# Relevance products behind the first six projections, the key search begun between them, and the bias matrix read back with a row step

## What is computed

```python
def block(i):
    ...
    rel = jax.nn.relu(jnp.einsum("bqhe,bse->bqhs", qi, k_idx).astype(jnp.float32))
    score = jnp.einsum("bqhs,bqh->bqs", rel, wi)
    ...
    score = jnp.where(causal[None], score, -jnp.inf)
    _, idx = lax.top_k(score, n_sel)
    ...
    bias = rel_bias[_t5_bucket(t[None, :, None] - idx)]
    logits = logits + jnp.transpose(bias, (0, 3, 1, 2)).astype(jnp.float32)
```

## Time and profile before

| | us |
|---|---|
| median of 3 runs | 2497.31 (2497.22 to 2499.72) |
| the profiled execution's span | 2496.9 |
| TensorE busy | 2376.4 (95%) |
| VectorE busy | 831.4 (33%) |
| ScalarE busy | 728.9 (29%) |
| GpSimd busy | 682.1 (27%) |

### The profile page before, as it was taken

One profiled execution on the slowest core, in us unless ns is written; L12 is line 12 of the kernel. 1 busy time (PEld: TensorE's weight loads), 2 busy tenths in 40 slices (PEclk: granted clock), 3 DMA queues, 4 the chain that ended last, 5 costly groups with the idle time before them and its releaser, 6 DMA issues.

```text
span 2496.9 us, 29386 instructions
## 1 busy us (share of the span) xinstructions
PE 2376.4 (95%) x11620; PEld 1715.4 (69%) x11620; DVE 831.4 (33%) x1298; ACT 728.9 (29%) x1089; POOL 682.1 (27%) x366
## 2 busy tenths in 40 slices
PE   7999999979999999989999999999999999999998
PEld 5585445753333347855899999979777677878875
DVE  2653412341111232350274054145000443721722
ACT  3324433321111211354142122232322334322222
POOL 3140012511111001110134444424433034544541
PEclk9699999989999999999999999999999999999999
DMA  4121111547899522200122222222222022322220
GB/s 152 60 93 59 46 37 40 229 165 273 356 358 380 237 68 72 76 18 9 59 85 85 93 86 84 93 85 94 93 85 76 18 75 69 101 85 97 97 89 38
DMA packets 68315, 275.41 MB, mean 110 GB/s; under 512 B 12488, under 2 KB 12616, under 8 KB 55920
## 3 DMA queue, kind: packets, MB, share of 16 engines
q1 hardware_dynamic: 59408, 259.61, 29.2%
q0 software_dynamic: 8512, 13.89, 1.6%
q10 hardware_dynamic: 288, 0.40, 0.1%
HBM read 321.02 MB, written 16.80 MB: 135 GB/s over the span
## 4 chain that ended last, share of the span: by engine, by line
PE 88%; issue 4%; DVE 3%; ACT 2%; POOL 2%; DMA 0%; DVEq 0%; POOLq 0%; SPq 0%; ACTq 0%
PE ps L826 16%; PE ps L809 15%; PE ps L1244 7%; PE ps L795 6%; PE ps L1016 4%; PE ps L1059 3%; PE ps L496 3%; PE ps L1266 3%; PE ps L1119 2%; PE ps L1205 2%; PE ps L707 2%; POOL weights_low L2473 2%; PE ps L1043 2%; PE ps L627 2%; PE ps L507 2%
## 5 line engine op out<-in xcount | busy, mean ns | idle before, releaser
L2473 POOL TENSOR_TENSOR weights_low<-weights,parts 128x1024 fp32r<-128x1024 f32 x218 | 547.3, 2513 | 988.4 <-ACT parts L1736 988.4
L826 PE MATMUL ps<-parts 128*128 128x512 f32 x1344 | 419.6, 392 | 9.2 <-DVE parts L2004 6.8
L809 PE MATMUL ps<-parts 128*128 128x264 f32 x2240 | 411.3, 285 | 8.1 <-DVE parts L2004 6.9
L1736 ACT ACTIVATE parts<-weights 128x1024 fp32r<-128x1024 f32 x218 | 229.1, 1055 | 440.4 <-PE ps L809 145.0
L809 PEld LDWEIGHTS ps<-parts 128*128 128x128 f32 x2240 | 349.6, 190 | 8.8 <-issue 8.7
L809 PE MATMUL ps<-parts,weights_low 128*128 128x264 f32 x1120 | 319.3, 285 | 0.0
L826 PEld LDWEIGHTS ps<-parts 128*128 128x128 f32 x1344 | 253.8, 189 | 66.1 <-issue 10.4
L826 PE MATMUL ps<-parts,weights_low 128*128 128x512 f32 x672 | 263.6, 392 | 0.0
L809 PEld LDWEIGHTS ps<-parts,weights_low 128*128 128x128 f32 x1120 | 213.1, 190 | 0.0
L1244 PE MATMUL ps<-area,normed 128*64 128x512 f32 x752 | 171.3, 597 | 1.6 <-DVE normed L2191 1.6
L2004 DVE TENSOR_TENSOR parts<-normed,parts 128x528 f32 (+1 forms) x64 | 152.2, 2378 | 10.1 <-DVE normed L2003 2.7
(11 more groups left out here) (419 smaller groups left out, 3307.7 us busy)
## 6 DMA issues: line engine op xcount, KB each, us to landing
weights<-in_weights SPq DMA_DIRECT2D x283, 512.0 KB, 3.4
area<-in_experts SPq DMA_DIRECT2D x141, 1024.0 KB
area<-pair_rows SPq DMA_DIRECT2D x4, 1024.0 KB, 8.1
residual<-in_x SPq DMA_DIRECT2D x4, 512.0 KB, 7.2
area<-bias_scratch POOLq DMA_DIRECT2D x1, 2048.0 KB, 9.7
token_rows<-area SPq DMA_DIRECT2D x1, 2048.0 KB, 6.6
out_tiles<-residual SPq DMA_DIRECT2D x4, 512.0 KB, 2.8
area<-in_decay POOLq DMA_DIRECT2D x2, 528.0 KB, 3.7
```

The costliest lines, as they stand in the source:

```text
L809: ins = mm(ps[:, b + h, 0:HALF], wt[:, k], x[:, m * DT + k, HALF * h:HALF * h + HALF], start=m == k == j == 0, stop=m == chunks - 1 and k ...
L826: ins = mm(ps[:, b], wt[:, k], x[:, m * DT + k, first:first + SEQ], start=m == k == j == 0, stop=m == chunks - 1 and k == DT - 1 and j == 2)
L1736: fn(high_slot(n, place), RING[:, n % SLOTS], ACT.Copy).then_inc(S["w_hi"], 1)
L2473: g.tensor_tensor(RING_LOW[:, n % SLOTS], RING[:, n % SLOTS], high_slot(n, place), ALU.subtract).then_inc(S["w_lo"], 1)
```

## The change

Five things change. The relevance products (`relevance`, four per call) stand behind the projections 1 to 6 of the twelve; they use banks 4 to 7 and four tiles `REL`. ScalarE's ReLUs stand behind the high part of the same turn. VectorE puts 5 rounds of the search for t = 1 behind its scoring steps 12, 16 and 20, and before the first of them waits for `bias_rows` and for the mask of t = 1. The bias vectors are written to DRAM from ScalarE's queue, each 128 times (`bias_scratch` is 8 x 128 x 640), and GpSimd reads the matrix from them with a step of 639 values from row to row, right into `BIAS`, so the reversed identity, its products and their copies are gone. And GpSimd makes the low parts of chunks 8 and 9 ahead of its wait for the write, those of 10 to 15 between its masks.

```diff
@@ -195,14 +195,14 @@
-        REL = [area(TMP, 512), area(TMP + 512, 512)]
+        REL = [area(TMP + 512 * j, 512) for j in range(4)]
...
-        BIAS_FLIPPED = area(5120, HEADS, SEQ)
-
+        RELS = [(t, h) for t in range(1, QT) for h in range(HEADS)]
+        EACH = 4
@@ -325,7 +325,7 @@
-        bias_scratch = nc.dram_tensor("bias_scratch", (HEADS, BIAS_W), F32, kind="Internal")
+        bias_scratch = nc.dram_tensor("bias_scratch", (HEADS, P, BIAS_W), F32, kind="Internal")
@@ -540,26 +540,13 @@
                              RELB, HOT[:, j * (BIAS_W // 2):(j + 1) * (BIAS_W // 2)], start=True, stop=True)
                 ins.then_inc(S["bias_vec"], 1)
 
-                if w.counted("act_evac"):
-                    pe.wait_ge(S["act_evac"], w.value("act_evac"))
-                for n, (t, h) in enumerate((t, h) for t in range(1, QT) for h in range(HEADS)):
-                    if n == 0:
+                begin_stage("act_evac")
+                for c in range(12):
+                    linear_split(HH, HL, IN_FIRST)
+                    if c == 0:
                         pe.wait_ge(S["bias_dram"], w.next("bias_dram", 1))
-                    if n >= 2:
-                        pe.wait_ge(S["rel_sb"], w.next("rel_sb"))
-                    r = slice(HD * (h % 2), HD * (h % 2) + HD)
-                    mm(ps[:, 4 + n % 2, 0:P * (t + 1)], QI[r, h // 2, P * t:P * t + P], KI[r, 0:P * (t + 1)],
-                       start=True, stop=True).then_inc(S["rel_done"], 1)
-                pe.wait_ge(S["rel_sb"], w.next("rel_sb", 2))
-                pe.wait_ge(S["bias_rows"], w.next("bias_rows", 16))
-                for h in range(HEADS):
-                    if h >= 2:
-                        pe.wait_ge(S["bias_flip"], w.next("bias_flip"))
-                    mm(ps[:, 4 + h % 2], FLIP, BIAS_FLIPPED[:, h], start=True, stop=True).then_inc(S["flip_done"], 1)
-                pe.wait_ge(S["bias_flip"], w.next("bias_flip", 2))
-                begin_stage("act_evac")
-                for _ in range(12):
-                    linear_split(HH, HL, IN_FIRST)
+                    relevance(range(EACH * c, min(EACH * c + EACH, len(RELS))))
+                pe.wait_ge(S["rel_sb"], w.next("rel_sb", 4))
                 banks = [bank() for _ in range(QT)]
                 for m in range(4):
                     wh, wl = (x.rearrange("p k c -> p (k c)") for x in take_parts(IN_FIRST))
@@ -779,6 +766,16 @@
                 pe_mlp(linear_tokens, [(0, 0, SEQ)], (XH1, XL1), (FH1, FL1))
                 layer_norm(TOKENS)
 
+            def relevance(turns):
+
+                for n in turns:
+                    t, h = RELS[n]
+                    r = slice(HD * (h % 2), HD * (h % 2) + HD)
+                    if n >= 4:
+                        pe.wait_ge(S["rel_sb"], w.next("rel_sb"))
+                    mm(ps[:, 4 + n % 4, 0:P * (t + 1)], QI[r, h // 2, P * t:P * t + P], KI[r, 0:P * (t + 1)],
+                       start=True, stop=True).then_inc(S["rel_done"], 1)
+
             def linear2(chunks, rhs, kts, fresh=None, late=False):
 
                 b = 2 * bank()
@@ -1348,18 +1345,18 @@
                 act.wait_ge(S["bias_vec"], w.next("bias_vec"))
                 fn(BVEC[:, 0:BIAS_W // 2], ps[0:HEADS, 6, 0:BIAS_W // 2], ACT.Copy)
                 fn(BVEC[:, BIAS_W // 2:], ps[0:HEADS, 5, 0:BIAS_W // 2], ACT.Copy).then_inc(S["bias_dram"], 1)
-                for n, (t, h) in enumerate((t, h) for t in range(1, QT) for h in range(HEADS)):
-                    act.wait_ge(S["rel_done"], w.next("rel_done"))
-                    if n >= 2:
-                        act.wait_ge(S["rel_used"], w.next("rel_used"))
-                    fn(REL[n % 2][:, 0:P * (t + 1)], ps[:, 4 + n % 2, 0:P * (t + 1)], ACT.Relu).then_inc(S["rel_sb"], 1)
-                w.count("rel_used", 2)
-                for h in range(HEADS):
-                    act.wait_ge(S["flip_done"], w.next("flip_done"))
-                    fn(BIAS[:, h], ps[:, 4 + h % 2], ACT.Copy).then_inc(S["bias_flip"], 1)
+                act.wait_ge(S["bias_dram"], 1)
+                act.dma_start(bias_scratch.ap(), BVEC.unsqueeze(1).to_broadcast([HEADS, P, BIAS_W])).then_inc(S["bvec_out"], 16)
                 for n, out in enumerate([x[:, j] for x in (QA, QB, KB) for j in range(4)]):
                     evac(out, bank(n), scale=QK_SCALE if n < 8 else 1.0)
                     high(n + 8, place=IN_FIRST, slots=-1)
+                    for m in range(EACH * n, min(EACH * n + EACH, len(RELS))):
+                        act.wait_ge(S["rel_done"], w.next("rel_done"))
+                        if m >= 4:
+                            act.wait_ge(S["rel_used"], w.next("rel_used"))
+                        keys = P * (RELS[m][0] + 1)
+                        fn(REL[m % 4][:, 0:keys], ps[:, 4 + m % 4, 0:keys], ACT.Relu).then_inc(S["rel_sb"], 1)
+                w.count("rel_used", 4)
                 for n in (20, 21):
                     high(n, place=IN_FIRST)
                 for t in range(QT):
@@ -1846,30 +1843,40 @@
                         .then_inc(S["dve_evac"], 1)
                 dve.wait_ge(S["dve_evac"], w.next("dve_evac", 2))
                 rms(1, SEQ, "kv_norm", lambda t: CKV, lambda t: CKV)
-                for t in range(1, QT):
-                    for h in range(HEADS):
-                        dve.wait_ge(S["rel_sb"], w.next("rel_sb"))
-                        rel, scalar = REL[((t - 1) * HEADS + h) % 2][:, 0:P * (t + 1)], WI[:, 8 * t + h:8 * t + h + 1]
-                        if h == 0:
-                            ins = v.tensor_scalar(SCORES[t], rel, scalar, None, ALU.mult)
-                        else:
-                            ins = v.scalar_tensor_tensor(out=SCORES[t], in0=rel, scalar=scalar, in1=SCORES[t],
-                                                         op0=ALU.mult, op1=ALU.add)
-                        ins.then_inc(S["rel_used"], 1)
-                        dve.wait_ge(S["rel_used"], w.next("rel_used"))
-
-                dve.wait_ge(S["bias_rows"], w.next("bias_rows", 16))
                 top = SMALL[:, 16:24]
-                for t in range(1, QT):
-                    dve.wait_ge(S["score_cut"], w.next("score_cut"))
-                    for _ in range(N_SEL // 8):
+
+                def largest_keys(t, times):
+                    for _ in range(times):
                         step(v.max(top, SCORES[t]))
                         step(v.match_replace(out=SCORES[t], in_to_replace=top, in_values=SCORES[t], imm_value=TAKEN))
+
+                def chosen_keys(t):
                     step(v.tensor_scalar(MASKS[t], SCORES[t], TAKEN, NEG, ALU.not_equal, ALU.mult))
+
+                for n, (t, h) in enumerate(RELS):
+                    dve.wait_ge(S["rel_sb"], w.next("rel_sb"))
+                    rel, scalar = REL[n % 4][:, 0:P * (t + 1)], WI[:, 8 * t + h:8 * t + h + 1]
+                    if h == 0:
+                        ins = v.tensor_scalar(SCORES[t], rel, scalar, None, ALU.mult)
+                    else:
+                        ins = v.scalar_tensor_tensor(out=SCORES[t], in0=rel, scalar=scalar, in1=SCORES[t],
+                                                     op0=ALU.mult, op1=ALU.add)
+                    ins.then_inc(S["rel_used"], 1)
+                    dve.wait_ge(S["rel_used"], w.next("rel_used"))
+                    if n == 11:
+                        dve.wait_ge(S["bias_rows"], w.next("bias_rows", 16))
+                        dve.wait_ge(S["score_cut"], w.next("score_cut"))
+                    if n in (11, 15, 19):
+                        largest_keys(1, 5)
+                largest_keys(1, N_SEL // 8 - 15)
+                chosen_keys(1)
+                for t in range(2, QT):
+                    dve.wait_ge(S["score_cut"], w.next("score_cut"))
+                    largest_keys(t, N_SEL // 8)
+                    chosen_keys(t)
                 dve.wait_ge(S["act_evac"], w.next("act_evac", 30))
                 w.count("tile_done", 30 - 6)
                 dve.wait_ge(S["score_mask"], w.next("score_mask"))
-                dve.wait_ge(S["bias_flip"], w.next("bias_flip", 8))
                 dve_dsa()
                 dve_stick()
 
@@ -2347,18 +2354,19 @@
                 pool.dma_start(WIDX, a["w_idx"]).then_inc(S["small_in"], 16)
                 for n in range(2, 8):
                     low(n, IN_FIRST)
-                pool.wait_ge(S["bias_dram"], w.next("bias_dram"))
-                pool.dma_start(bias_scratch.ap(), BVEC).then_inc(S["bvec_out"], 16)
+                for n in (8, 9):
+                    low(n, IN_FIRST)
                 pool.wait_ge(S["bvec_out"], w.next("bvec_out", 16))
-                rows = bass.AP(bias_scratch, 0, [[1, P], [BIAS_W, HEADS], [1, SEQ]])
-                pool.dma_start(BIAS_FLIPPED, rows).then_inc(S["bias_rows"], 16)
-                pool.wait_ge(S["bias_rows"], w.next("bias_rows", 16))
+                rows = bass.AP(bias_scratch, P - 1, [[BIAS_W - 1, P], [P * BIAS_W, HEADS], [1, SEQ]])
```

(5 more changed lines are left out.)

10 lines of the change are left out of this document (5 added, 5 removed).

## The result

The changed kernel takes **2515.2 us** in the median of five executions (2510.2 to 2535.6); the kernel before took 2499.7 beside it. The ratio over all their executions is 1.0077, with a 95% interval of 1.0049 to 1.0106; by the two medians it is slower by 15.5 us. One execution of the kernel before, 4661 us beside vector_wait_late, is left out of that run's ratio. The forecast was 2504.8 with a range of 2483 to 2520. The sign and the mechanism came out, the size did not: the loss is twice what was forecast, and the time lies outside the 2500.8 to 2509.8 that I had given the likeliest case by itself.

The account below looks back on a forecast made before the run. TensorE's chain was taken as the bound (88% of 2496.9 us). Write landing 124.0 + 58.0 ends the twelfth projection at 182.0 against 174.5, 7.5 us later: 2497.3 + 7.5 = 2504.8 us, range 2483 to 2520.

Parts of the forecast that it names:

- the likeliest case: The slow write from 8 partitions, landing at 120 to 129 us, gives 2500.8 to 2509.8 us in total; chance 0.58.
- The chain's bound and the free run: TensorE's path sets the time; if nothing else is late, the twelfth projection ends at 154.0 us, 20.5 us gained.
- One term: Relevance products behind the first six projections, priced from full-clock 128x512 products: 15.5 us in all.
- (d): Rival: relevance products, 64 rows deep, keep TensorE's clock low through six projections, costing some 45 us if unhidden; chance 0.04.
- The write: Bias vectors, 2.62 MB out of 8 partitions at 51 GB/s: 51.4 us moving, first bytes after 1.1, landing at 124.0.
- Rival (a): The bias write is fast, half the read's rate: 15.1 us, landing at 87.7, the whole 20.5 us gained, 2476.8; chance 0.16.
- (b): Rival: the bias write at a rate between, 80 GB/s, lands at 105.4, 11.1 us gained, 2486.2; chance 0.08.
- GpSimd's wait: GpSimd waits for the bias write until 124.0, its low part is ready at 128.1; TensorE stands 24.7 us before projection five.
- VectorE's wait and chain: VectorE waits for the read (9.7 us, landing 133.8), then 23.6 us of rounds and steps, plus 0.3 of hand-overs.
- The term that was mis-sized: Projections nine to twelve, started at 160.4 by GpSimd's low part, take 4 x 5.47 = 21.9 us; the twelfth ends at 182.0.
- Carried one for one: The twelfth projection's delay, 7.5 us, reaches the kernel's end unchanged, since nothing behind it starts at a fixed time.
- The search hidden: VectorE's search ends near 205 us, the attention first uses it at 214, so the search costs nothing.

Follow-up runs that it names:

- vector_wait_late: Changed kernel with VectorE's wait for the read back moved behind its search, the write and GpSimd's wait left alone: 2507.3 us, ratio 1.0034 to the kernel before.
- wide_write: Changed kernel with the bias vectors made 16 times over 128 partitions, each partition written 8 times: 2477.6 us, ratio 0.9934 to the kernel before.
- spread_source: Changed kernel with the 8 source rows of the write at partitions 0, 4, 8 to 28 instead of 0 to 7: 2476.2 us, ratio 0.9912.
- spread_by_8: Changed kernel with the 8 source rows of the write at partitions 0, 8, 16 to 56 instead of 0 to 7: 2489.8 us, ratio 0.9964.
- spread_wider: Changed kernel with the 8 source rows of the write at partitions 0, 16, 32 to 112 instead of 0 to 7: 2490.5 us, ratio 0.9982.
- late_waits: Changed kernel, slow write kept, with GpSimd's wait and read behind chunk 15's low part and VectorE's wait behind the search: 2473.8 us, ratio 0.9907.
- no_early_rounds: Changed kernel with all 16 search rounds for t = 1 behind the 24 scoring steps again, VectorE's wait unmoved: 2509.1 us, ratio 1.0046.
- both_fixes: Changed kernel with the write from 128 partitions and also GpSimd's and VectorE's waits moved behind the low parts and the search: 2477.8 us, ratio 0.9930.

## Why the prediction was right, and where it was off

- **The chain's bound and the free run**: right in kind. Without the waits the twelfth projection ends at 147.0 (three kernels), 27.5 us before the old 174.5; I had 154.0, 20.5 us. One term was too dear. The relevance products cost 1.06, 1.49 and 1.92 us for each four (the chains above show 1.06 and 1.92, `L776 x8`), 8.9 us in all against 15.5: the heads lie alternately in partitions 0 to 63 and 64 to 127, and neighbouring 64-row products took 0.56 to 0.62 of what I had scaled from the 128-row products of the earlier trace rows. I argued in (d) with their depth and did not use it in the price. Of the other 0.4 us, the stage began earlier (at 69.11 in wide_write, for 70.70) and the projections took 1.1 us more than 65.6 + 2.2.
- **The write**: right in kind and nearly in size, 55.1 us from issue for 52.5. Taking the old write's 51 GB/s as a rate, though it moved but 20 KB, was the choice that carried the forecast; the runs of the table show it to be a property of where the 8 rows lie. That the moving itself came out to the tenth (51.5 us for 51.4) is partly luck: in the trace of before the eight rows took 0.10 to 0.32 us each, a row of the new write 0.35 in the mean. The miss is the start, 3.0 us from issue to first bytes where I had 1.1, and 0.6 from the last byte to the end of GpSimd's wait, which I had left out.
- **Rival (a)** needed 8 engines to be what 8 rows give. spread_source is that case (18.4 us, 2476.2 for the 2476.8 I had worked out), only not with neighbouring rows. **(b)** is spread_by_8 and spread_wider: landed at 100.2 and 99.2, 2489.8 and 2490.5 us, where (b) said 105.4 and 2486.2.
- **GpSimd's wait**: as predicted (38.3 us idle, fifth projection released by the low part that ends near 129.7). TensorE stood 31.3 us ahead of it and not 24.7, since it came there sooner; as VectorE was later still, that did not count.
- **VectorE's wait and chain**: as predicted, 10.15 for the read (9.7), then 23.9 us from the first round to the last step (23.6 + 0.3).
- **The term that was mis-sized** is the last one, 4 x 5.47 = 21.9 us for the last four projections. They took 24.50. I charged TensorE's second stand, ahead of the ninth projection, as time alone, though I had put 2.15 us of half clock on the first stand; the granted clock was 0.64 from 162 to 170. Together: 1.05 earlier, 2.6 from the write, 0.35 from the read, 0.3 from hand-overs, 2.9 from this term (the 2.6, and the 0.3 that I had taken off it): 187.1 for 182.0.
- **Carried one for one**: failed by about 5 us. The 12.6 us at 188 us are 13.0 at 444, 15.4 at 559, 16.1 at 590 and 17.5 near 963 us; vector_wait_late, whose profile has no dip near 1100 us, goes from 4.6 at 180 to 8.1 at 582 and 9.0 at the end. Half of it is lost in a few products of TensorE, here before and in the changed kernel:

```profile
541.26 0.89 PE ps L659 x8
```

```profile
554.81 1.71 PE ps L646 x8
```

The granted clock was 0.93 from 540 to 544 us before, and 0.54 from 553 to 559 in the changed kernel: it falls in both kernels near here, in the one behind these products and in the other among them. In late_waits and no_early_rounds they take the 0.89 of before, in wide_write and vector_wait_late 1.71, and there late_waits and wide_write part, from 0.4 us at 404 to 3.5 at 547. What sets this isn't settled: it goes with when the stage is reached, and no run here changes that alone. With it 7.5 + 5.1 + 4.9 is 17.5 over the 2496.9 of before, 2514.4; the spans of the executions without the dip are 2508.5 to 2514.1.
- **The search hidden**: right for the changed kernel, and no_early_rounds shows by how little: without early rounds it costs 4.6 us at 215 us.

## What to carry to other kernels

A DMA's size says little where its source is small: look at which partitions it reads, and lay a row that is sent many times on partitions that do not share a way out (here a step of 4 made 55 us into 18, and a step of 8 only into 29). From there on the number of rows counts: 128 source rows in place of 8 made 18 into 11. Before mending a slow transfer, move its waits to the first use: here that alone gave everything, 2473.8 us against 2515.2. And when a stall is costed, each separate stand of TensorE is worth its length and 1.4 to 3.1 us of lower clock behind it (7.10 for 5.66 us in vector_wait_late's chain; 24.96 for 21.9 in spread_by_8's).

## What the runs showed that I had not expected

- A step of 16 partitions is slower than a step of 12 or 4 (29.3, 18.5 and 18.4 us): spreading further is no improvement by itself.
- The slow write holds up others. The weight loads issued beside it took 15.3 us in the median in the changed kernel and 13.6 in late_waits, where wide_write and spread_source had 3.5 (512 KB each). Nothing waited for them here, since they are issued early enough. The rows, of the changed kernel and of wide_write:

```profile
weights<-in_weights SPq DMA_DIRECT2D x4, 512.0 KB, 15.3
```

```profile
weights<-in_weights SPq DMA_DIRECT2D x9, 512.0 KB, 3.5
```

- Two 64-row f32 products in different halves of the rows overlap: in late_waits each begins within 7 ns of its neighbour. Four 128x256 take 1.06 us at full clock, four 128x512 1.92.
- Single executions differ by a dip of some 17 us near 1050 to 1140 us. both_fixes had three of eight at 2494 to 2495 and five at 2476 to 2478; its profile shows 0.86 and 0.54 for the clock between 1020 and 1100 where late_waits had 1.00 and 0.91. A single execution could have turned the sign of a 15 us effect.
